# Reordering the mixing stage of a diffusion layer: query latent first, gate projection last with the retention woven in

## What is computed

```python
rq, rk, rv, rg, cq, ckv, kr = split(h @ w_in)     # 512, 512, 1024, 1024, 512, 256, 64 columns
q  = rms_norm(cq, q_norm_g) @ w_uq                # 8 heads of 128 + 64 (rotary)
kv = rms_norm(ckv, kv_norm_g) @ w_ukv             # 8 heads of 128 + 128
# retention: 8 heads, dk 64, dv 128, both directions; keys of context and latent,
# weight gamma**distance per head and direction, rotary on rq and rk
y  = retention(rotate(rq), rotate(rk), rv)        # latent queries only
y  = (y - mean(y)) * rsqrt(var(y) + 1e-5)         # over the 128 values of a head and token
ret_out = silu(rg) * y
mla_out = softmax(q @ k.T * 192**-0.5) @ v        # k: 128 from kv, 64 rotary from kr
x  = x + gate * (concat(ret_out, mla_out) @ w_out)
```

## Time and profile before

| | us |
|---|---|
| runs shown, median (3 runs: 3024.62, 3028.65, 3033.72) | 3028.65 |
| profiled execution, its own time | 3024.51 |
| its span, first to last instruction | 3022.7 |
| PE busy | 2856.8 |
| DVE busy | 1688.9 |
| ACT busy | 907.2 |
| mean granted TensorE clock | 0.969 |

### The profile page before, as it was taken

One profiled execution on the slowest core, in us unless ns is written; L12 is line 12 of the kernel. 1 busy time (PEld: TensorE's weight loads), 2 busy tenths in 40 slices (PEclk: granted clock), 3 DMA queues, 4 the chain that ended last, 5 costly groups with the idle time before them and its releaser, 6 DMA issues.

```text
span 3022.7 us, 33655 instructions
## 1 busy us (share of the span) xinstructions
PE 2856.8 (95%) x13271; PEld 2351.0 (78%) x13271; DVE 1688.9 (56%) x1665; ACT 907.2 (30%) x846; POOL 7.0 (0%) x15
## 2 busy tenths in 40 slices
PE   4889999999999999999999699887989999999998
PEld 3668888888888888888877698655688888888886
DVE  5656757465665756565656632274465555555556
ACT  5441212122121212212113432233345333333334
POOL 0000000000000000000000000000000000000000
PEclk9899999999999999999999799987999999999999
DMA  7756646455554657667664353301244555555553
GB/s 252 244 183 202 187 120 188 125 159 166 149 163 132 190 157 255 195 217 224 199 188 132 98 154 97 110 15 56 70 153 154 182 193 187 188 194 183 192 187 133
DMA packets 426445, 496.78 MB, mean 164 GB/s; under 512 B 19090, under 2 KB 302088, under 8 KB 425608
## 3 DMA queue, kind: packets, MB, share of 16 engines
q1 hardware_dynamic: 425880, 493.20, 52.4%
q0 software_dynamic: 496, 2.63, 0.3%
HBM read 493.69 MB, written 2.10 MB: 164 GB/s over the span
## 4 chain that ended last, share of the span: by engine, by line
PE 82%; DVE 5%; ACT 3%; issue 2%; DMA 1%; SPq 0%; ACTq 0%; DVEq 0%
PE py L908 8%; PE py L910 8%; PE py L909 8%; PE pg L908 5%; PE pg L910 5%; PE pg L909 5%; PE pu L908 4%; PE pu L910 4%; PE pu L909 4%; PE py L1313 2%; PE py L1315 2%; PE py L1314 2%; ACT wh L557 2%; PE pg L1294 1%; PE pg L1296 1%
## 5 line engine op out<-in xcount | busy, mean ns | idle before, releaser
L1385 DVE TENSOR_TENSOR wl<-raw,wh 128x2048 fp32r<-128x2048 f32 x342 | 782.6, 2292 | 914.2 <-ACT wh L557 913.7
L557 ACT ACTIVATE wh<-raw 128x2048 fp32r<-128x2048 f32 x342 | 653.2, 1914 | 1325.7 <-PE py L910 451.5
L908 PE MATMUL py<-ah,wh 128*128 128x512 f32 x704 | 278.7, 396 | 4.4 <-DVE xy L1531 3.3
L910 PE MATMUL py<-ah,wl 128*128 128x512 f32 x704 | 276.8, 393 | 0.0
L909 PE MATMUL py<-al,wh 128*128 128x512 f32 x704 | 276.6, 393 | 0.0
L908 PE MATMUL pu<-hh,wh 128*128 128x512 f32 x656 | 255.9, 390 | 0.0
L908 PE MATMUL pg<-hh,wh 128*128 128x512 f32 x656 | 255.5, 389 | 0.0
L910 PE MATMUL pu<-hh,wl 128*128 128x512 f32 x656 | 255.3, 389 | 0.0
L910 PE MATMUL pg<-hh,wl 128*128 128x512 f32 x656 | 255.2, 389 | 0.0
L909 PE MATMUL pu<-hl,wh 128*128 128x512 f32 x656 | 255.2, 389 | 0.0
L909 PE MATMUL pg<-hl,wh 128*128 128x512 f32 x656 | 255.2, 389 | 0.0
(11 more groups left out here) (376 smaller groups left out, 4777.9 us busy)
## 6 DMA issues: line engine op xcount, KB each, us to landing
raw<-in_ffn_w_in SPq DMA_DIRECT2D x170, 1024.0 KB
chunk<-in_ada_w SPq DMA_DIRECT2D x189, 512.0 KB, 3.9
raw<-in_ffn_w_out SPq DMA_DIRECT2D x88, 1024.0 KB
raw<-in_ada_w SPq DMA_DIRECT2D x64, 512.0 KB
raw<-in_mix_w_in SPq DMA_DIRECT2D x30, 1024.0 KB
accc<-in_ada_w SPq DMA_DIRECT2D x35, 512.0 KB, 4.6
raw<-in_mix_w_out SPq DMA_DIRECT2D x16, 1024.0 KB
war<-in_ffn_w_in SPq DMA_DIRECT2D x16, 384.0 KB, 3.9
```

The lines of the kernel that those rows point to most:

```text
L557: nc.scalar.activation(wh[:, slot % 2, :], raw[:, slot, :], ACT.Copy).then_inc(wh_ready, 1)
L908: mm(out_ap, w[0], xh_ap, start=first, stop=False, skip_group_check=True)
L910: return mm(out_ap, w[1], xh_ap, start=False, stop=last, skip_group_check=True)
L1385: tt(wl[:, slot % 2, :], raw[:, slot, :], wh[:, slot % 2, :].bitcast(F32), ALU.subtract).then_inc(wl_ready, 1)
```

## The change

The slabs are renumbered: CQ first, RG last before UQ. CQ (and RG) become row slabs like RV. The first loops of PE, ACT and DVE are written anew with the splits inside; PE's projection loops are written out; RQ0 and RQ1 go to banks pa and pb, the rest from RQ2 on round py. The norms of cq and ckv and the rotations move in between the slabs. The gate projection (tokens stationary, 512 gate columns moving, banks pg and pu) is cut by slab around the retention heads. Decayed scores are written over decay and are now the stationary operand of `ret_values`, so that y has tokens on partitions; mean and variance are DVE's bn_stats and bn_aggr; y is turned back by 16 transposes. Silu of the gate is one ACT operation over 128x2048. The last rotations move ahead of the v up-projection. The core of it, with the buffers' new places and the semaphores' names left out:

```diff
-S_RG, S_CQ, S_RQ, S_CKV, S_KR, S_RK, S_RV = 0, 8, 12, 16, 18, 19, 23
+S_CQ, S_RQ, S_CKV, S_KR, S_RK, S_RV, S_RG = 0, 4, 8, 10, 11, 15, 23
 # SP
-            in_slabs(S_RG, C_RG, HEADS)
-            in_slabs(S_CQ, C_CQ, QT)
+            row_slabs(S_CQ, C_CQ)
...
+            for half in range(2):
+                row_slabs(S_RG + 4 * half, C_RG + half * 512)
 # POOL
-            pool.wait_ge(slab_used, MIX0 + S_UQ)
+            pool.wait_ge(slab_used, MIX0 + S_RG)
             pool.dma_start(far[:]...)
 # ACT
+            for t in range(KT):
+                hh_tile(0, 0, ml[:, 3 * KT:4 * KT], t)
+                if t in (7, 11, 15):
+                    static_split(MIX0 + 2 + (t - 7) // 4)
+            for j in range(QT):
+                project(S_CQ + 3, cq[:, j, :], py[j][:, 0:LAT])
+            nc.scalar.activation(lsq[:], cq[:]..., ACT.Square).then_inc(lsq_ready, 1)
+            for t in range(KT):
+                hh_tile(0, 1, mc[:, 3 * KT:4 * KT], t)
+                if t in (2, 6, 10, 14):
+                    j = (t - 2) // 4
+                    static_split(MIX0 + S_RQ + j + 1)
+                    if j:
+                        project(S_RQ + j - 1, ...)
...
+            for h in range(HEADS - 1):
+                if h == 3:
+                    gates_out(0)
+                static_split(MIX0 + S_RG + h + 2)
+                if h == 4:
+                    values_out(0)
+                if 1 <= h:
+                    decays(h + 1)
+            se.wait_ge(rs_done, HEADS)
             nc.scalar.activation(cqh[:], cq[:], ACT.Copy).then_inc(cqh_ready, 1)
+            static_split(MIX0 + S_UQ + 1)
+            se.wait_ge(decay_ready, HEADS)
             nc.scalar.activation(ckvh[:], ckv[:], ACT.Copy).then_inc(cqh_ready, 1)
+            gates_out(1)
+            values_out(1)
+            nc.scalar.activation(rg[:]..., rg[:]..., ACT.Silu).then_inc(rgs_ready, 1)
+            se.wait_ge(yst_ready, 2)
+            nc.scalar.activation(ysd[:, 0], ymv[:, :, :, 1], ACT.Sqrt, bias=eps[:, 1:2], scale=1.0).then_inc(ysd_ready, 1)
+            for half in range(2):
+                for h in range(4 * half, 4 * half + 4):
+                    up(h, qn[:, h, :], py[h % 4][:, 0:LAT])
+                static_split(MIX0 + S_UQ + half + 2)
+            for k in range(4):
+                y_high(k)
 # PE
+            for s in range(4):
+                pe.wait_ge(wl_ready, MIX0 + S_CQ + s + 1)
+                for j in range(4):
+                    t = 4 * s + j
+                    pe.wait_ge(hl_ready, TILES[0] + t + 1)
+                    for c_ in range(QT):
+                        ins = three(py[c_][:, 0:LAT], w_at(s, j * 512 + c_ * P, ...), hh[:, 0, t, :], hl[:, 0, t, :], ...)
+                ins.then_inc(slab_used, 1)
...
             def ret_values(h):
-                for j in range(4):
-                    ins = mm(pab[h % 2][:, 0:LAT], rv[:, j, h * P:(h + 1) * P], pret[:, h % 2, j, :], ...)
+                for k in range(2):
+                    for j in range(4):
+                        ins = mm(pab[k][:, (h % 4) * P:(h % 4 + 1) * P], decay[:, h % 2, j, k * P:(k + 1) * P], rv[:, j, h * P:(h + 1) * P], ...)
+            gate_slab(0)
+            pe.wait_ge(proj_free, S_RV + 8)
             ret_scores(0)
+            for h in range(1, HEADS - 1):
+                gate_slab(h)
+                ret_scores(h)
+                ret_values(h - 1)
+            ret_scores(HEADS - 1)
+            ret_values(HEADS - 2)
+            gate_slab(HEADS - 1)
+            ret_values(HEADS - 1)
+            pe.wait_ge(lat_split, 1)
+            up_queries(0)
+            up_queries(1)
+            pe.wait_ge(yn_ready, 1)
+            for k in range(4):
+                y_turn(k)
+            up_queries(2)
...
+            pe.wait_ge(mixl_ready, 4)
+            for j in range(4):
+                swap(9 + j, qr[:, j, :], 2)
             m = MIX0 + S_UKV + 1
 # DVE
+            for h in range(HEADS - 1):
+                static_split(MIX0 + S_RG + h + 2)
+                weigh(h)
+                if h >= 1:
+                    ve.wait_ge(ry_done, h)
+                    decay_arg(h + 1)
+                if h == 5:
+                    value_stats(0)
+            weigh(HEADS - 1)
             ve.wait_ge(cqh_ready, 1)
             tt(cql[:], cq[:], cqh[:].bitcast(F32), ALU.subtract).then_inc(lat_split, 1)
+            static_split(MIX0 + S_UQ + 1)
             ve.wait_ge(cqh_ready, 2)
             tt(ckvl[:], ckv[:], ckvh[:].bitcast(F32), ALU.subtract).then_inc(lat_split, 1)
+            value_stats(1)
+            static_split(MIX0 + S_UQ + 2)
+            ve.wait_ge(ysd_ready, 1)
+            link(nc.vector.reciprocal(ysd[:, 1], ysd[:, 0]))
+            for k in range(2):
+                for h in range(HEADS):
+                    y = yret[:, k, h * P:(h + 1) * P]
+                    ins = ts(y, y, ymv[:, k, h, 0:1], ysd[:, 1, k, h:h + 1], ALU.subtract, ALU.mult)
+            link(ins)
+            ve.wait_ge(rgs_ready, 1)
+            for k in range(2):
+                ins = tt(yret[:, k, :], yret[:, k, :], rg[:, k, :], ALU.mult)
+            ins.then_inc(yn_ready, 1)
```

More of the change, by code:

```diff
@@ new lines, in _ @@
+            value_banks = [py[(k + 1) % 4] for k in range(4)]
+            for half in range(2):
+                for q in range(4):
+                    s = S_RV + 4 * half + q
+                    pe.wait_ge(wl_ready, MIX0 + s + 1)
+                    if q == 0:
+                        pe.wait_ge(proj_free, S_RV + 4 * half)
+                    row_slab(s, value_banks, 4 * q).then_inc(slab_used, 1)
+                    if half == 0 and q < 2:
+                        swap(6 + q, rk[:, 2 + q, 0:LAT], 1)
+                    if half == 0 and q == 2:
+                        swap(8, krope[:, 0:LAT], 2)
@@ new lines, in latent_norm @@
+            def latent_norm(k):
+                ve.wait_ge(lrms_ready, k + 1)
+                n, t_, row, r = ((QT, cq, V_QG, rms[:, 0:LAT]), (CT, ckv, V_KG, rms[:]))[k]
+                link(nc.vector.reciprocal(r, r))
+                for t in range(n):
+                    ins = stt(t_[:, t, :], t_[:, t, :], vt[:, row + t:row + t + 1], r, ALU.mult, ALU.mult)
+                ins.then_inc(lat_normed, 1)
+            static_split(MIX0 + S_CKV + 1)
+            latent_norm(0)
+            rotate(0, rq[:, 0, :], 0)
@@ L1673, in decay_arg, with weigh, value_stats @@
                 stt(d, far[:, 0, 0:2, :], lg[:, h:h + 1], d, ALU.mult, ALU.add).then_inc(darg_ready, 1)
+            def weigh(h):
+                ve.wait_ge(decay_ready, h + 1)
+                link(tt(decay[:, h % 2, 2:4, :], decay[:, h % 2, 2:4, :], dback[:, h % 2], ALU.add))
+                ve.wait_ge(rs_done, h + 1)
+                for j in range(2):
+                    d = decay[:, h % 2, 2 * j:2 * j + 2, :]
+                    ins = stt(d, py[2 * (h % 2) + j][:].rearrange("p (a b) -> p a b", a=2), float(DK) ** -0.5, d, ALU.mult, ALU.mult)
+                ins.then_inc(rp_ready, 1)
+            def value_stats(half):
+                ve.wait_ge(ry_free, half + 1)
+                heads = [(k, h) for k in range(2) for h in range(4 * half, 4 * half + 4)]
+                for k, h in heads:
+                    ins = nc.vector.bn_stats(yst[:, k, h, :], yret[:, k, h * P:(h + 1) * P])
+                link(ins)
+                for k, h in heads:
+                    ins = nc.vector.bn_aggr(ymv[:, k, h, :], yst[:, k, h, :])
+                ins.then_inc(yst_ready, 1)
             ve.wait_ge(far_loaded, 16)
```

436 lines of the change are left out of this document (183 added, 253 removed).

## The result

| | before | after |
|---|---|---|
| median of the runs, us (4 runs each, same chip) | 3029.86 | 2960.11 |
| lowest and highest | 3024.62 to 3033.72 | 2956.96 to 2963.85 |
| profiled execution, own time / span | 3024.51 / 3022.7 | 2956.96 / 2955.1 |
| PE, DVE, ACT busy | 2856.8, 1688.9, 907.2 | 2826.8, 1676.6, 898.8 |
| mean granted clock | 0.969 | 0.982 |

What follows compares the result with a forecast made beforehand. PE was taken as the bound, busy nine tenths of nearly every slice, so its waits were priced: 61.4-8.5+6.8+10.1 = 69.8, less 2.8 for restarts, 67 us saved. From 3028.65 that gave 2961.7 us, range 2950 to 2985.

Steps and rivals of the forecast that it cites:

- fourteen restarts of PE: Remaining waits that restart PE, estimated at 0.2 us each as the pipeline fills anew: 2.8 us off the gain.
- Part 1: Mixing stage up to CKV, latent queries first, splits inside tile loops: 57.9 us against 119.3, 61.4 saved.
- Part 2: CKV to the end of the values, with norms and rotations put in between: 174.1 us against 165.6, 8.5 lost.
- Part 3: Gate projection woven with retention heads: 75.5 us together, values 14.2 of it, first values waiting 2.3 us.
- Part 4: Behind the values to the first attention score: with the woven heads 132.7 us against 139.5, 6.8 saved.
- Both gaps: PE's two waits in part 4: UQ1 waits 2.7 us, then 5.1 us for DVE's normalising and gate products.
- Part 5: First attention step: full clock since V, not the swaps, ends the stage; 18.4 us against 28.5, 10.1 saved.
- Table switches: ACT's table loads: 1.28 us each, next operation 0.01 later; the skill's drain would lengthen part 4's chain by 2.8 us.
- rival C: Dearer ACT table switches in part 4, 1.28 us more for each of two: gain 64, 2964 us; chance 0.03.
- Rival D: PE's straight-line code not fed, slower beyond 2.5 us per block for 31 slabs; 3055 us at 3; chance 0.03.
- Rival E: No gain: woven stage stays at half clock, gates, scores and values double (+73), 3035 us; chance 0.02.
- rival B: Splits and tail chain bind harder, bn work dear, half clock in part 4, cold attention step: gain 40, 2989; chance 0.15.

Runs made afterwards that it cites:

- all4: Changed kernel with new tail order, weighing before splits, last swaps within the k up-projection, matmuls of ones, and value banks awaited singly: 2931.59 us, ratio 0.9680.
- banks: Changed kernel with ACT copying the last key bank out before a split and PE waiting for each value bank by itself: 2955.04 us, ratio 0.9753.
- weigh_first: Changed kernel with DVE weighing each head's scores before it splits the next gate slab: 2952.19 us, ratio 0.9746.
- tail: Changed kernel with ACT reordered behind the last gate slab, and DVE's UQ2 split and ckvl behind norm and gate products: 2947.74 us, ratio 0.9724.
- tail_dve: Changed kernel with only DVE's split of UQ2 moved behind the norm and gate products, ACT's order kept: 2950.59 us, ratio 0.9747.
- swaps_late: Changed kernel with the last four swaps and rotations put back behind the v up-projection: 2973.0 us, ratio 0.9805.
- splits_behind: Changed kernel with the seven splits put back behind the latent and context tile loops: 2974.17 us, ratio 0.9812.
- rot_late: Changed kernel with the first nine swaps and rotations moved back behind the value slabs, norms left in place: 2965.79 us, ratio 0.9782.
- unweave: Changed kernel with all eight gate slabs ahead of the eight retention heads: 2966.77 us, ratio 0.9784.
- control: The changed kernel itself, run again beside three variants and the kernel before: 2954.82 us, ratio 0.9762.
- warm: Changed kernel with extra, unread matmuls of ones in the two waits ahead of the mixing stage: 2958.49 us, ratio 0.9769.

## Why the prediction was right

The forecast was 2961.7 us, the median 2960.1. By parts the forecast is 383.1 us and the measurement 385.5, so the mechanism held, but the closeness of the total is in part luck: errors cancel inside parts 1 and 4, and the 2.4 us that are left were covered by the 2.8 us put down for fourteen restarts of PE at 0.2 us. No row here shows such a restart by itself, at this price or another. (A slip in the reading of the earlier trace rows had no part in the sum: slice 29 is at 9, so the exceptions are slices 23, 26 to 28 and 30.)

- **Part 1**, forecast 57.9, measured 56.3. Right in size, by two errors that cancel. The waits were 3.5 us (0.7, 2.5, 0.3) and not 8.2. The half clock was dearer than 1.7: PE was busy 52.8 us, where all4 needs 49.0 at full clock, so it cost 3.8 of work, of which 2.6 reach the end of the stage. DVE took 6.9 us for four context tiles and a split, not 6.0, as it waits 1.06 us for ACT's copy in each.
- **Part 2**, forecast 174.1, measured 174.3; the two waits of 2.3 came as 2.2 and 2.2. banks shows that they were for ACT's order and one coarse wait.
- **Part 3**, forecast 75.5 to the last values, measured 79.8. This is the term that was mis-sized. The values took 1.98 us a head, not the 1.78 of the nearest row (a pair of operands that no row showed), and the first head 3.7, since the wait of 2.2 that was forecast brought half clock with it, which was not. A 0.6 us wait at the last head was missed too. These are 1.6, 1.7 and 0.6 of the 4.3 us by which the forecast fell short. weigh_first took 4.6 us back: the forecast wait of 2.2, its half clock, and the 0.6. I had named the queue behind that wait ("a split ahead of the first weighing") and not asked whether it had to stand there.
- **Part 4**, forecast 57.2, measured 57.2 behind the last values. Both gaps came where they were placed: 2.6 for 2.7 and 4.2 for 5.1, the second released by DVE's yret as said. tail and tail_dve show the chain with its two engines. That the sum fits so well is again cancelling: UQ1 took 7.5 us at half clock, 1.7 more than forecast; the wait for yret was 0.9 shorter; turns and UQ2 took 9.2 us with their half clock, not 11.7; and swaps, V and the last copy took 17.2, not 15.2, with half clock behind the swaps. bn_stats and bn_aggr were 3.3 and 1.3 us for both halves, within the bound and hidden.
- **Part 5**, forecast 18.4, measured 17.9 at clock 1.00; swaps_late takes it to 24.8.
- **Table switches**: 1.28 us each, the next operation 0.01 to 0.02 us behind. The drain that the Trainium skill adds (ScalarE: Activation LUTs, "What ACT_TABLE_LOAD costs") shows in none of the rows; rival C falls.
- **Rival D** falls: the straight code ran at 0.12 and 0.23 us a matmul, with no wait but those above. Rival E had no part in it. Of rival B one piece came, half clock behind every wait of the tail; its other terms did not.

Where the gain is can be read from both traces. The kernel before, from the end of RV to the first score, in three windows (norms and rotations, heads, group norm with the up-projections):

```profile
1951.20:1984.80 33.60, 17.57 (x32) 8.19 (x31) 24.86 (x54) 9.70 (x12) 0.54 (x1) 0.58 0.18 62
1984.80:2019.80 35.00, 34.06 (x128) 25.25 (x128) 24.99 (x40) 18.75 (x32) 0.00 (x0) 0.86 0.00 1
2019.80:2090.70 70.90, 53.03 (x264) 41.73 (x265) 42.32 (x39) 33.86 (x50) 0.00 (x0) 0.90 0.24 74
```

- **Up to CKV:** 119.3 us less the 46.1 of the gate slabs that moved is 73.2; it became 56.3. That saves 16.9, and splits_behind gives 17.1 back, so it is the woven splits.
- **Norms and rotations:** the 33.6 us are gone, and 8.7 came back between CKV and the gates, so 24.9 are saved. rot_late gives 10.4 back; the other 14 or so are by subtraction the norms of cq and ckv, whose chain (waits of 6.5, 1.5 and 5.4 us) stood in that window. No run moved the norms back, so this is not tested.
- **Heads with gates:** 35.0 + 46.1 became 79.8. That saves 1.3, and the gate slabs' new form is 2.5 by count (46.1 against 43.6). The woven heads are no faster than the old bare ones; the 9.7 us of unweave are what the new order would lose without the weaving.
- **Behind the values, with the first attention step:** 70.9 + 28.5 became 57.2 + 17.9. That saves 24.3. swaps_late gives 12.1 back; some 12 are left for the new group norm and the order around it, by subtraction. The old group norm in the new order was not tried.

Together that is 67.4 us.

## What to carry to other kernels

Where PE waits for an engine that serves in written order, list what stands ahead of the awaited operation and is itself waiting: moving one 2.3 us split behind it gave 4.6 us in the heads and some 6 in the tail, more than the wait that the profile shows, because a stretch at half clock goes with it. Move short chains of dependent work (norms, rotations) out of the place where nothing else is left for PE, in between dense work (projections) that doesn't wait for them, and keep the last items of a short chain off the end of a stage: four swaps there cost 12 us. Judge edits of a few microseconds by stage windows from a fixed event, when the start of the stage moves by 12 us between executions.

## What the runs showed of the hardware

The clock behind a wait is not the same in each execution. The windows just behind the 2.25 us wait between the value halves, with the same instructions up to there, in control and in tail:

```profile
1851.70:1855.70 4.00, 3.97 (x17) 3.30 (x18) 2.21 (x1) 2.97 (x2) 0.00 (x0) 1.00 0.00 0
```
```profile
1857.50:1861.50 4.00, 4.00 (x11) 3.19 (x12) 2.28 (x2) 2.90 (x2) 0.00 (x0) 0.60 0.00 0
```
Four profiles (tail, weigh_first, tail_dve and rot_late) lost 1.5 us there, the seven others with this wait none; the earlier trace rows had shown the harmless case only. Behind the 2.2 us wait for the first values (decay) the clock fell each time, but not for as long: from the first gate slab to the last values its mean was 0.98 and the time 79.8 us in the change, and 0.96 and 80.8 to 81.1 us in tail, tail_dve, banks and splits_behind, with the same instructions and waits. Behind the 2.6 us wait for qn it was 0.62 in the changed kernel and 1.00 in banks, tail_dve and splits_behind:

```profile
1983.25:1987.25 4.00, 4.00 (x33) 4.00 (x34) 1.49 (x1) 3.13 (x6) 0.00 (x0) 1.00 0.00 0
1994.90:1998.90 4.00, 4.00 (x19) 4.00 (x20) 3.86 (x4) 2.09 (x4) 0.00 (x0) 0.50 0.14 24
```

These are banks behind qn and behind yret; splits_behind had the 5.7 us wait and the longer stage (138.8) too. Where PE keeps its clock behind qn it reaches yret 1.5 us earlier and waits 5.7 instead of 4.2, since DVE sets that time; behind the longer wait the turns then ran at 0.50 for the whole of 4 us. That is 0.6 of the 2.0 us by which this stage was longer in banks; 1.3 lie ahead of the last values. Matmuls that nothing needs (0.23 us for one of ones, at full clock) filled two waits of some 4 us in warm and all4, and the clock was 1.00 there; in the other eleven profiles of the change and its variants, with those waits empty, it had fallen to half before the first matmul of the stage. Nor is it one price: behind the 2.5 us wait for the split of RQ1 the clock fell in warm and not in all4. What decides the fall of the clock in one execution and not in the next, and how long it lasts, stays open.
